# Ten pieces of the first mixer's input projection as 512-column products, with the halves joined in SBUF

## The chip, the cores and the metric

The kernel runs on one core of a Trainium2 chip. The metric is the device time of one execution in microseconds. The core's engines work side by side, each through its own queue in order, and wait for one another by semaphores: TensorE (PE) multiplies, VectorE (DVE) and ScalarE (ACT) work elementwise, GpSimd (POOL) does little here, SyncE (SP) issues the DMAs. PE writes to PSUM alone, which has eight banks of 512 float32 columns; in the programs they are called ps0 to ps7.

## The reference

Three residual blocks over 256 tokens of width 1024. What the change touches is the input projection of the first block's mixer:

```python
h = rmsnorm(x, norm_mix_g[i])
u = h @ w_in[i]
u_rwkv, u_attn, u_gate = jnp.split(u, [RWKV_COLS, RWKV_COLS + ATTN_COLS], axis=-1)
o_a = rwkv7_time_mix(u_rwkv, ...)   # first: c = c + (prev - c) * mu, over tokens
o_b = diff_attention(u_attn, ...)   # q * head_dim ** -0.5, k, v
g_a, g_b = jnp.split(jax.nn.sigmoid(u_gate), 2, axis=-1)
x = x + (g_a * (o_a @ w_proj_a[i]) + g_b * (o_b @ w_proj_b[i])) @ w_out[i]
```

`u_rwkv` has 1792 columns (r, k, v, the decay's, a's and gate's inner parts), `u_attn` 1536 (q, k, v), `u_gate` 2048. All is float32. After the mixer come a squared-ReLU feed-forward, a gate, and then two layers of SwiGLU feed-forward and attention.

## The kernel before

**Precision and weights.** A float32 matrix is split into a high part (ACT rounds it to PE's faster float32 form, L2581) and a low part (DVE subtracts, L2927). Every product is three: high by high, high by low, low by high. The weights come as a stream of pieces of 1 MB; three buffers each hold the raw piece, its high and its low part. A piece's cast waits until PE has used the piece three places before it, and its load until that one's low part is made.

**The stage.** `w_in` is done first in ten and one pieces of 256 columns, whose result is transposed (columns on partitions, tokens along the row): seven pieces for the RWKV inputs in the order of `RWKV_ORDER`, then four for q and k of the differential attention. The first has a form of its own. Each of the others is done by `cols_piece` (L666): 8 steps of contraction x 2 groups of 128 columns x 3 products of 256 tokens (L2072 high by high, L2073 weights' high by tokens' low, L2074 weights' low by tokens' high), all in one PSUM bank of 2 x 256. After every two steps of contraction it yields, so other work may stand there in PE's queue. Then follow v and the gates by `rows_mat` (512-column products with the tokens as the stationary side), and `w_proj_b`.

**Behind a piece.** Of an RWKV piece, DVE scales the bank by the tokens' norm into a buffer (`shift`, L3054), ACT writes the part of the token itself (`shift_old`, L2627 and L2628), and DVE adds the shifted part (`shift_add`, L3058 and L3059), after which `c_ready` counts one. Of a q or k piece, DVE scales the bank (`dqk`). From the first piece ACT makes the decay's inner part (`lora_in`, two table loads), PE two pairs of small products (`lora`, L2273 and L2274), ACT eight sigmoids of them (`lora_out`, L2640 and L2641). When three pieces are ready, ACT squares and copies the keys (`kk`, L2658 and L2662), and PE sums them over heads (`kk_sum`, L2282). From all that follows the RWKV chain: scores, products of 64 x 64, states, outputs.

**The order.** The program is written by generators. `weave` (L1120) runs them as tracks and takes the one whose engine is free first by a table of expected durations; `mixers_fill`, the projections, is the track that fills in. `take` hands out the PSUM bank that has been given back longest ago, and `give` returns it once its reader has been written down; on the chip the next writer then waits for that reader:

```python
def claim(sl):
    if sl.n > 1:
        e.wait_ge(free[sl.b], sl.n - 1)
```

**The wide form.** The feed-forward pieces are done by `wide_runs` (L713): one product of 512 columns takes the weights' high part against the tokens' high and low parts side by side (L2157), which fills a bank, and one of 256 adds the low weights (L2164). A piece takes two banks; its 32 products stand in PE's queue without a break: every other piece has 16 wide ones first and then its low ones, the pieces between begin with two wide ones. In the feed-forward stage ACT then copies one half of each bank to SBUF (L2777) and DVE adds the other half to it (L2920).

Of the kernel before, what the change touches and what calls it, by code (L numbers as in the profile page):

```python
# [14 lines left out]
S = 256  # L15
# [17 lines left out]
LEAD = 10.0  # L33
# [187 lines left out]
def program(nc, ws, xin, pin, colsin, constin, smallin, rowin, out):  # L221
# [4 lines left out]
    with ExitStack() as ctx:  # L226
        def sem(name):
            return ctx.enter_context(nc.semaphore(name))
# [28 lines left out]
        diag_ready = Sig(sem("diag_ready"))  # L257
        c_part = Sig(sem("c_part"))
# [1074 lines left out]


# [217 lines left out]
        def diff():  # L1552
            while "vd" not in state or "bonus" not in state:
                yield None
# [59 lines left out]

        def shifts():

            for n in range(len(RWKV_ORDER)):
                while len(to_shift) <= n:
                    yield None
                p, c, sl, at = to_shift[n]  # L1620
# [4 lines left out]
                emit("shift_old", act=0.83, slot=sl, c=c, i=p % 2, v=c_part.add())  # L1625
                yield "dve"
                emit("shift_add", dve=0.7, c=c, i=p % 2, v_part=c_part.n, v=c_ready.add())

        def mixers_fill(nm):
            for p, c in enumerate(RWKV_ORDER):  # L1630
                def shift(sl, c, nxt, p=p):
                    early.append((p, c, sl, cur[0]))
# [12 lines left out]

            def dq(sl, c, nxt):
                emit("dqk", dve=0.7, slot=sl, n=(c - 1792) // 128)
                if nxt:
                    emit_lo(nxt)
                state["dk"] = sl  # L1650

            for c in range(1792, 2816, 256):
                yield from cols_piece("w_in", 0, c, "h", nm.h_needs, dq)
# [39 lines left out]
        weave([shifts(), rwkv_decays(), rwkv_keys(), (rwkv_chain(), LEAD), (rwkv_block(0), LEAD), (rwkv_block(1), LEAD),  # L1693
# [359 lines left out]
        def tensor_program(e):  # L2053
# [27 lines left out]
            for s in script:  # L2081
# [349 lines left out]
                elif kind == "d_soft":  # L2431
# [3 lines left out]
                    if h == 0:  # L2435
                        read_out(state["dk"])
# [112 lines left out]
        def scalar_program(e):  # L2549
# [20 lines left out]
            for s in script:  # L2570
# [52 lines left out]

                elif kind == "shift_old":
                    read_out(sl)
# [256 lines left out]
        def vector_program(e):  # L2882
# [31 lines left out]

            def add_halves(s, to):
# [17 lines left out]
            for s in script:  # L2933
# [117 lines left out]
                elif kind == "shift":  # L3051
                    c, u_ = s["c"] // 128, ub[s["i"]]
                    ready(sl)
                    e.tensor_tensor(u_[:, :, 1:S + 1], b2(sl), RB2, ALU.mult).then_inc(free[sl.b], 1)  # L3054
# [206 lines left out]
                elif kind == "dqk":  # L3261
                    n = s["n"]
                    ready(sl)
                    if n < 4:
                        e.scalar_tensor_tensor(qT[:, n:n + 2, :], b2(sl), 0.125, RB2, ALU.mult,
                                               ALU.mult).then_inc(free[sl.b], 1)
                    else:
                        e.tensor_tensor(kTt[:, n - 4:n - 2, :], b2(sl), RB2, ALU.mult).then_inc(free[sl.b], 1)
# [381 lines left out]
```

## Time and profile before

| what | value |
|---|---|
| median of 3 runs | 1420.3 us (1419.92 to 1421.13) |
| the profiled execution | 1420.28 us |
| its span in the trace | 1418.5 us |
| PE busy | 1412.6 us, 9224 products |
| DVE, ACT busy | 1128.3 and 803.4 us |

The span runs from the first to the last instruction that the trace has. Products overlap in PE's pipeline, so what one costs is the distance of two starts, not its own length. "Idle" in the trace is time in which an engine had nothing in it; a row that has it names the engine that ended it.

### The profile page before, as it was taken

How to read it: one execution, taken by the hardware profiler on the slowest of the kernel's cores; microseconds unless marked ns; L12 is line 12 of the kernel's file. 1: busy time of each engine (PE TensorE's matmuls, PEld its weight loads, DVE VectorE, ACT ScalarE, POOL GpSimd, SP SyncE). 2: the span in 40 equal slices, each digit the busy share in tenths (PEclk: the TensorE clock that was granted, in tenths of full speed). 3: DMA queues.
4: the chain of work that ended last, by engine and by line, in shares of the span. 5: the costliest groups of instructions: out<-in, count | busy, mean ns of one | idle time of the engine just before them, and what ended most of it. 6: DMA issues, size and time to landing. Idle time of an engine off the chain costs nothing.

```text
span 1418.5 us, 22820 instructions
## 1 busy us (share of the span) xinstructions
PE 1412.6 (100%) x9224; PEld 1203.5 (85%) x9224; DVE 1128.3 (80%) x1543; ACT 803.4 (57%) x1084; POOL 26.3 (2%) x93
## 2 busy tenths in 40 slices
PE   9999999999999999999999999999999999999999
PEld 8988778888888888889878888888888887888887
DVE  6876776786448898888877888889888798688896
ACT  7735473654336565545866565555554557665552
POOL 0000000000001100000000000000000000000000
PEclk9999999999999999999999999999999999999999
DMA  9441325555554555555434555645555444355553
GB/s 339 149 150 62 113 102 204 201 204 187 203 178 179 179 198 189 178 207 178 150 119 166 190 189 188 218 161 199 200 183 193 165 177 149 110 202 194 181 179 115
DMA packets 36104, 249.11 MB, mean 176 GB/s; under 512 B 4128, under 2 KB 4256, under 8 KB 6688
## 3 DMA queue, kind: packets, MB, share of 16 engines
q1 hardware_dynamic: 35712, 247.46, 49.7%
q8 instruction: 74, 1.21, 0.4%
q10 hardware_dynamic: 288, 0.19, 0.1%
q14 instruction: 30, 0.25, 0.1%
HBM read 246.59 MB, written 1.05 MB: 175 GB/s over the span
## 4 chain that ended last, share of the span: by engine, by line
PE 97%; DMA 1%; ACT 1%; DVE 1%; issue 0%; SPq 0%; DVEq 0%; ACTq 0%
PE ps L2157 24%; PE ps L2072 16%; PE ps L2074 16%; PE ps L2073 16%; PE ps L2164 13%; PE ps L2147 2%; PE ps L2332 2%; DMA raw<-ws 1%; PE ps L2146 1%; PE ps L2246 1%; PE ps L2545 1%; PE ps L2525 1%; PE ps L2534 1%; PE ps L2317 0%; ACT hi L2581 0%; PE ps L2469 0%
## 5 line engine op out<-in xcount | busy, mean ns | idle before, releaser
L2927 DVE TENSOR_TENSOR lo<-raw,hi 128x2048 fp32r<-128x2048 f32 (+1 forms) x230 | 525.1, 2283 | 109.9 <-ACT hi L2581 106.9
L2581 ACT CAST hi<-raw 128x2048 fp32r<-128x2048 f32 (+1 forms) x230 | 438.6, 1908 | 205.5 <-PE ps L2074 143.0
L2157 PE MATMUL ps<-h,hi 128*128 128x512 f32 x1504 | 359.2, 390 | 0.0
L2157 PEld LDWEIGHTS ps<-h,hi 128*128 128x128 f32 x1504 | 276.4, 188 | 52.4
L2072 PE MATMUL ps<-hi,a 128*128 128x512 f32 x552 | 218.6, 396 | 0.0
L2074 PE MATMUL ps<-hi,a 128*128 128x512 f32 x552 | 215.4, 390 | 0.0
L2073 PE MATMUL ps<-lo,a 128*128 128x512 f32 x552 | 215.1, 390 | 0.0
L2164 PEld LDWEIGHTS ps<-h,lo 128*128 128x128 f32 x1504 | 192.2, 190 | 7.9
L2164 PE MATMUL ps<-h,lo 128*128 128x256 f32 x1504 | 194.4, 282 | 0.0
L2777 ACT COPY a<-ps 128x256 f32<-128x256 f32 x208 | 76.4, 372 | 178.3 <-PE ps L2157 89.2
L2072 PEld LDWEIGHTS ps<-hi,a 128*128 128x128 f32 x552 | 103.7, 188 | 22.9 <-issue 2.4
L2074 PEld LDWEIGHTS ps<-hi,a 128*128 128x128 f32 x552 | 103.6, 188 | 22.0
L2073 PEld LDWEIGHTS ps<-lo,a 128*128 128x128 f32 x552 | 103.8, 188 | 20.7
L2072 PE MATMUL ps<-hi,h 128*128 128x512 f32 x272 | 112.0, 412 | 0.0
L2074 PE MATMUL ps<-hi,h 128*128 128x512 f32 x272 | 106.3, 391 | 0.0
L2073 PE MATMUL ps<-lo,h 128*128 128x512 f32 x272 | 106.2, 390 | 0.0
L2920 DVE TENSOR_TENSOR a<-ps,a 128x256 f32<-128x256 f32 x208 | 82.6, 420 | 18.7 <-ACT a L2777 16.8
L2072 PE MATMUL ps<-h,hi 128*128 128x256 f32 x224 | 64.8, 289 | 0.4 <-DVE lo L2927 0.4
L2073 PE MATMUL ps<-h,hi 128*128 128x256 f32 x224 | 63.4, 283 | 0.0
L2074 PE MATMUL ps<-h,lo 128*128 128x256 f32 x224 | 63.3, 283 | 0.0
L2072 PEld LDWEIGHTS ps<-hi,h 128*128 128x128 f32 x272 | 51.1, 188 | 12.2 <-issue 2.3
L2074 PEld LDWEIGHTS ps<-hi,h 128*128 128x128 f32 x272 | 51.1, 188 | 11.1
(385 smaller groups left out, 1713.7 us busy)
## 6 DMA issues: line engine op xcount, KB each, us to landing
raw<-ws SPq DMA_DIRECT2D x229, 1024.0 KB, 4.8
X<-xin SPq DMA_DIRECT2D x8, 256.0 KB, 5.3
raw<-ws SPq DMA_DIRECT2D x2, 512.0 KB, 6.2
out<-X SPq DMA_DIRECT2D x4, 256.0 KB, 2.1
small<-small SPq DMA_DIRECT2D x1, 992.5 KB, 12.3
const<-const SPq DMA_DIRECT2D x1, 900.0 KB, 6.6
a<-row SPq DMA_DIRECT2D x1, 512.0 KB, 7.2
const<-const SPq DMA_DIRECT2D x1, 388.0 KB, 12.7
```

The costliest lines, as they stand in the source:

```text
L2072: e.matmul(o, ah, bh, start=start, stop=False)
L2073: e.matmul(o, ah, bl, start=False, stop=False)
L2074: return e.matmul(o, al, bh, start=False, stop=stop)
L2146: e.matmul(b2(sl)[:, 0, :], wl[:, k, a:a + 128], HH[:, k, :], start=False, stop=False)
L2147: t = e.matmul(b2(sl), wh[:, k, a:a + 128], h2[:, k, :, :], start=False, stop=k == 7)
L2157: t = e.matmul(b2(s["slots"][u]), wh[:, k, 128 * u:128 * u + 128], h2[:, k, :, :], start=k == 0, stop=last)
L2164: t = e.matmul(b2(s["slots"][u])[:, 0, :], wl[:, k, 128 * u:128 * u + 128], HH[:, k, :], start=False, stop=last)
L2332: t = e.matmul(banks[z.b][half(q ^ n), 64 * h:64 * h + 64], TB[blk][l][half(q), h, :], TB[blk][r][half(q), h, :], start=True, stop=True)
L2581: e.copy(hi[j % NSPL][:, n], raw[j % NRAW][:, n]).then_inc(hi_ready, 1)
L2777: e.copy(half_to[s["to"]][s["j"]][:, s["u"], :], b2(sl)[:, 1, :]).then_inc(half_a.sem, 1)
L2920: e.tensor_tensor(to[:, u, :], b2(x)[:, 0, :], half_to[kind][j][:, u, :], ALU.add).then_inc(free[x.b], 1)
L2927: e.tensor_tensor(lo[j % NSPL][:, n], raw[j % NRAW][:, n], hi[j % NSPL][:, n].bitcast(F), ALU.subtract).then_inc(lo_ready, 1)
```

## The change

Ten pieces, all RWKV ones but the first and the four of q and k, go from `cols_piece` to `wide_runs`. Their results lie in two banks as two halves each. A new step `halves` (ACT, L2667 of the changed kernel) copies the second half of each bank into one of two buffers `hv`; `meet_halves` (DVE, L2963) adds the first half, which frees the bank; the scaling by the tokens' norm is then done in SBUF (L3107, L3323). `shift_old` waits for a new semaphore, `piece_scaled`. The buffers `hv` share their place with some of the RWKV chain's, so the chain's blocks may be written down only after the last piece of k (`"dk"`), and so may the differential attention.

```diff
+        hv_ar = Arena(vend + 3 * 16 * S)
+        hv = [hv_ar([128, 2, S]) for _ in range(2)]
...
         def rwkv_block(blk):
+            while "dk" not in state:
+                yield None
...
+        def halves_out(n, slots, at):
+
+            yield "act", at
+            emit("halves", act=0.9, slots=slots, i=n % 2, over=state.get(("hv", n % 2)), v=[half_a.add() for _ in slots])
+            halves = script[-1]["v"]
+            state["hv", n % 2] = slots[1]
+            return halves
...
+        def queries():
+
+            for n in range(4):
+                while len(to_scale) <= n:
+                    yield None
+                c, sl, other, at = to_scale[n]
+                halves = yield from halves_out(7 + n, (other, sl), at)
+                yield "dve"
+                emit("dqk", dve=1.4, slot=sl, other=other, halves=halves, i=(7 + n) % 2, n=(c - 1792) // 128, v=scaled_v.add())
+                for x in (other, sl):
+                    give(x)
+            state["dk"] = scaled_v.n
...
-                yield "dve", at
-                emit("shift", dve=0.55, slot=sl, c=c, i=p % 2)
-                give(sl)
+                p, c, sl, other, at = to_shift[n]
+                halves = None
+                if other:
+                    halves = yield from halves_out(p, (other, sl), at)
+                    yield "dve"
+                else:
+                    yield "dve", at
+                emit("shift", dve=1.35 if other else 0.55, slot=sl, other=other, halves=halves, c=c, i=p % 2, v=scaled_v.add())
...
-                    yield from cols_piece("w_in", 0, c, "h", nm.h_needs, shift)
+                    yield from wide_runs("w_in", 0, c, nm.h_needs, no_begin, shift)
...
-                yield from cols_piece("w_in", 0, c, "h", nm.h_needs, dq)
+                yield from wide_runs("w_in", 0, c, nm.h_needs, no_begin, dq)
...
-        weave([shifts(), rwkv_decays(), rwkv_keys(), (rwkv_chain(), LEAD), (rwkv_block(0), LEAD), (rwkv_block(1), LEAD),
+        weave([shifts(), queries(), rwkv_decays(), rwkv_keys(), (rwkv_chain(), LEAD), (rwkv_block(0), LEAD), (rwkv_block(1), LEAD),
...
+                elif kind == "halves":
+                    if s["over"]:
+                        read_out(s["over"])
+                    for u, x in enumerate(s["slots"]):
+                        ready(x)
+                        e.copy(hv[s["i"]][:, u, :], b2(x)[:, 1, :]).then_inc(half_a.sem, 1)
                 elif kind == "shift_old":
-                    read_out(sl)
+                    e.wait_ge(scaled_v.sem, s["scaled"])
...
+            def meet_halves(s, to):
+
+                for u, x in enumerate((s["other"], s["slot"])):
+                    e.wait_ge(half_a.sem, s["halves"][u])
+                    e.tensor_tensor(to[:, u, :], b2(x)[:, 0, :], hv[s["i"]][:, u, :], ALU.add).then_inc(free[x.b], 1)
+                read_out(s["other"])
+                read_out(s["slot"])
...
+                    if s["other"]:
+                        meet_halves(s, u_)
+                        e.tensor_tensor(u_, u_, RB2, ALU.mult).then_inc(scaled_v.sem, 1)
...
+                    meet_halves(s, t)
+                    e.scalar_tensor_tensor(t, t, 0.125 if n < 4 else 1.0, RB2, ALU.mult, ALU.mult).then_inc(scaled_v.sem, 1)
```

The order of the queues shows it best around the small products of the decay and the keys. PE before, from the first pair of decay products to the first key sum; `small` holds the decay's weights, `a1` the mixed inputs, `a14` the keys' squares:

```order
L2074 MATMUL ps1<-h_59,lo0_55 128x256
L2273 MATMUL ps2<-a1_67,small_62 128x256 [waits const_in,rwkv_act,bank_free3,bank_free2]
L2274 MATMUL ps3<-a1_67,small_62 128x256
...
L2273 MATMUL ps4<-a1_67,small_62 128x256 [waits const_in,rwkv_act,bank_free7,bank_free4]
L2274 MATMUL ps7<-a1_67,small_62 128x256
...
L2282 MATMUL ps2<-a14_80,const_61 128x256 [waits rwkv_keys,bank_free2]
L2072 MATMUL ps6<-h_59,hi2_54 128x256
```

PE now, from the end of piece 3 to the start of piece 5:

```order
L2202 MATMUL ps4<-h_59,lo0_55 128x256 x8
L2311 MATMUL ps0<-a1_67,small_62 128x256 [waits const_in,rwkv_act,bank_free5,bank_free0]
L2312 MATMUL ps5<-a1_67,small_62 128x256
...
L2195 MATMUL ps6<-h_59,hi1_53 128x512 [waits hi_ready,bank_free7,bank_free6]
...
L2195 MATMUL ps7<-h_59,hi1_53 128x512 x7
L2311 MATMUL ps1<-a1_67,small_62 128x256 [waits const_in,rwkv_act,bank_free2,bank_free1]
L2312 MATMUL ps2<-a1_67,small_62 128x256
...
L2320 MATMUL ps0<-a14_80,const_61 128x256 [waits rwkv_keys,bank_free0]
...
L2195 MATMUL ps5<-h_59,hi2_54 128x512 [waits hi_ready,bank_free3,bank_free5]
```

Before, the pairs of decay products stand two steps of contraction apart, inside piece 3, and the key sums two pieces later inside piece 5. Now a whole piece lies between the pairs, and the first key sum follows the second pair at once, in the first pair's bank.

ACT before, from the cast of piece 5 to the squares of the keys; `hi` are casts, `a9` and `a12` the sigmoids of the decay products:

```order
L2581 CAST hi2_54<-raw2_51 128x2048 [waits bank_full0,raw_in2]
L2627 ACTIVATE a1_67<-a3_69,st_63 128x256 [waits bank_free6]
L2640 ACTIVATE a9_75<-ps2,cols_60 128x256 [waits bank_full3]
...
L2641 ACTIVATE a12_78<-ps7,cols_60 128x256
L2627 ACTIVATE a1_67<-a2_68,st_63 128x256 [waits bank_free0]
...
L2581 CAST hi0_52<-raw0_49 128x2048 [waits bank_full1,raw_in0]
...
L2658 ACTIVATE a14_80<-a1_67,st_63 128x256 [waits c_ready]
```

ACT now, from the same cast to the sigmoids:

```order
L2619 CAST hi2_54<-raw2_51 128x2048 [waits bank_full2,raw_in2]
L2671 ACTIVATE a1_67<-a3_69,st_63 128x256 [waits piece_scaled]
...
L2619 CAST hi0_52<-raw0_49 128x2048 [waits bank_full4,raw_in0]
L2667 COPY a33_99<-ps1 128x256 [waits bank_full1]
...
L2671 ACTIVATE a1_67<-a2_68,st_63 128x256 [waits piece_scaled]
...
L2702 ACTIVATE a14_80<-a1_67,st_63 128x256 [waits c_ready]
...
L2619 CAST hi1_53<-raw1_50 128x2048 [waits bank_full7,raw_in1]
L2667 COPY a34_100<-ps3 128x256 [waits bank_full3,bank_free7]
...
L2684 ACTIVATE a9_75<-ps0,cols_60 128x256 [waits bank_full5]
L2685 ACTIVATE a12_78<-ps5,cols_60 128x256
```

The eight sigmoids stood ahead of the casts of the pieces 6 and 7 and ahead of the keys' squares and copies; now they stand behind all of these.

## Rows read from the trace of the kernel before

**Rows 1.** The page: busy times, and the granted clock in 40 slices.
```profile
PE 1412.6 (100%) x9224; PEld 1203.5 (85%) x9224; DVE 1128.3 (80%) x1543; ACT 803.4 (57%) x1084; POOL 26.3 (2%) x93
...
PEclk9999999999999999999999999999999999999999
```

**Rows 2.** Waits of PE, 12 to 200 us: us in total, times, longest.
```profile
PE ps L2072 <- DVE lo L2927: 0.4, 1, 0.4
PE ps L2273 <- ACT a L2633: 0.2, 1, 0.2
```

**Rows 3.** Windows: us; PE, PEld, DVE, ACT, POOL busy; clock, DMA share, GB/s.
```profile
16.00:84.00 68.00, 67.36 (x640) 65.20 (x641) 54.42 (x70) 46.95 (x63) 2.24 (x9) 1.00 0.57 203
```

**Rows 4.** Timeline of PE in piece 2: start, length in us, what.
```profile
23.09 0.28 PE L2072 MATMUL ps<-h,hi 128*128 128x256 f32 x1
...
29.81 0.28 PE L2074 MATMUL ps<-h,lo 128*128 128x256 f32 x1
```

**Rows 5.** Timeline of PE in the first feed-forward stage.
```profile
289.71 6.99 PE L2157 MATMUL ps<-h,hi 128*128 128x512 f32 x30
296.54 2.08 PE L2164 MATMUL ps<-h,lo 128*128 128x256 f32 x16
298.45 0.63 PE L2157 MATMUL ps<-h,hi 128*128 128x512 f32 x2
```

**Rows 6.** Timeline of PE: start of piece 1, first decay products, and behind.
```profile
16.43 0.38 PE L2072 MATMUL ps<-h,hi 128*128 128x256 f32 x1 [0.43 <-DVE lo L2927]
...
30.30 0.45 PE L2273 MATMUL ps<-a,small 64*128 64x256 f32 x1 [0.21 <-ACT a L2633]
...
31.36 0.39 PE L2072 MATMUL ps<-h,hi 128*128 128x256 f32 x1
```

**Rows 7.** The page's groups: busy us, mean ns, idle before.
```profile
L2777 ACT COPY a<-ps 128x256 f32<-128x256 f32 x208 | 76.4, 372 | 178.3 <-PE ps L2157 89.2
...
L2920 DVE TENSOR_TENSOR a<-ps,a 128x256 f32<-128x256 f32 x208 | 82.6, 420 | 18.7 <-ACT a L2777 16.8
```

**Rows 8.** Timeline of DVE behind the pieces 1 and 2.
```profile
29.74 0.69 DVE L3054 TENSOR_TENSOR a<-ps,RB 128x512 f32<-128x512 f32 x1
...
34.19 0.48 DVE L3058 SCALAR_TENSOR_TENSOR a<-a,cols,a 128x256 f32<-128x256 f32 x1
...
34.98 0.68 DVE L3054 TENSOR_TENSOR a<-ps,RB 128x512 f32<-128x512 f32 x1
```

**Rows 9.** Timeline of DVE in the first feed-forward stage.
```profile
291.12 0.69 DVE L3304 TENSOR_TENSOR a<-a,a 128x512 fp32r<-128x512 f32 x1 [0.69 <-ACT a L2781]
```

**Rows 10.** Timeline of ACT, 24 to 48 us.
```profile
25.80 0.51 ACT L2627 ACTIVATE a<-a,st 128x256 f32<-128x256 f32 x1
...
26.73 1.28 ACT L2632 ACT_TABLE_LOAD   x1
...
30.06 1.88 ACT L2581 CAST hi<-raw 128x2048 fp32r<-128x2048 f32 x1
31.85 0.51 ACT L2627 ACTIVATE a<-a,st 128x256 f32<-128x256 f32 x1
...
32.66 0.45 ACT L2640 ACTIVATE a<-ps,cols 128x256 f32<-128x256 f32 x1
33.02 0.46 ACT L2641 ACTIVATE a<-ps,cols 128x256 f32<-128x256 f32 x1
...
40.61 1.70 ACT L2658 ACTIVATE a<-a,st 128x256 f32<-128x256 f32 x4
...
43.81 1.89 ACT L2581 CAST hi<-raw 128x2048 fp32r<-128x2048 f32 x1
```

**Rows 11.** Timeline of the program's first PE work.
```profile
1.44 3.78 PE L2079 MATMUL ps<-lo 128*128 128x512 f32 x8 [1.44 <-DVE lo L2932]
...
10.02 0.28 PE L2100 MATMUL ps<-h,hi 128*128 128x256 f32 x1
...
10.13 0.28 PE L2101 MATMUL ps<-h,hi 128*128 128x256 f32 x1
```

More of the change, by code:

```diff
@@ L257, in program @@
         diag_ready = Sig(sem("diag_ready"))
+        scaled_v = Sig(sem("piece_scaled"))
         c_part = Sig(sem("c_part"))
@@ L1552, in diff @@
         def diff():
-            while "vd" not in state or "bonus" not in state:
+            while "vd" not in state or "bonus" not in state or "dk" not in state:
                 yield None
@@ L1619, in shifts, with no_begin, shift @@
                     yield None
-                p, c, sl, at = to_shift[n]
-                yield "dve", at
-                emit("shift", dve=0.55, slot=sl, c=c, i=p % 2)
-                give(sl)
+                p, c, sl, other, at = to_shift[n]
[6 more added lines that the diff above has]
+                emit("shift", dve=1.35 if other else 0.55, slot=sl, other=other, halves=halves, c=c, i=p % 2, v=scaled_v.add())
+                scaled = scaled_v.n
+                for x in (other, sl):
+                    if x:
+                        give(x)
                 yield "act"
-                emit("shift_old", act=0.83, slot=sl, c=c, i=p % 2, v=c_part.add())
+                emit("shift_old", act=0.83, scaled=scaled, c=c, i=p % 2, v=c_part.add())
                 yield "dve"
                 emit("shift_add", dve=0.7, c=c, i=p % 2, v_part=c_part.n, v=c_ready.add())
+        def no_begin(sl, c, u):
+            pass
         def mixers_fill(nm):
             for p, c in enumerate(RWKV_ORDER):
-                def shift(sl, c, nxt, p=p):
-                    early.append((p, c, sl, cur[0]))
+                def shift(sl, c, nxt, other=None, p=p):
+                    early.append((p, c, sl, other, cur[0]))
                     if p == 1:
@@ L1643, in mixers_fill, with dq @@
                 else:
-                    yield from cols_piece("w_in", 0, c, "h", nm.h_needs, shift)
[L1646 to L1650, printed above, removed]
+                    yield from wide_runs("w_in", 0, c, nm.h_needs, no_begin, shift)
+            def dq(sl, c, nxt, other):
+                to_scale.append((c, sl, other, cur[0]))
+                emit_lo(nxt)
+                return True
             for c in range(1792, 2816, 256):
-                yield from cols_piece("w_in", 0, c, "h", nm.h_needs, dq)
+                yield from wide_runs("w_in", 0, c, nm.h_needs, no_begin, dq)
             def vd(sl, b, h):
@@ L3051, in vector_program @@
                 elif kind == "shift":
-                    c, u_ = s["c"] // 128, ub[s["i"]]
-                    ready(sl)
-                    e.tensor_tensor(u_[:, :, 1:S + 1], b2(sl), RB2, ALU.mult).then_inc(free[sl.b], 1)
+                    c, u_ = s["c"] // 128, ub[s["i"]][:, :, 1:S + 1]
+                    if s["other"]:
+                        meet_halves(s, u_)
+                        e.tensor_tensor(u_, u_, RB2, ALU.mult).then_inc(scaled_v.sem, 1)
+                    else:
+                        ready(sl)
+                        e.tensor_tensor(u_, b2(sl), RB2, ALU.mult).then_inc(free[sl.b], 1)
+                        read_out(sl)
+                        e.sem_inc(scaled_v.sem, 1)
                 elif kind == "shift_add":
@@ L3262, in vector_program @@
                     n = s["n"]
[L3263 to L3268, printed above, removed]
+                    t = qT[:, n:n + 2, :] if n < 4 else kTt[:, n - 4:n - 2, :]
+                    meet_halves(s, t)
+                    e.scalar_tensor_tensor(t, t, 0.125 if n < 4 else 1.0, RB2, ALU.mult, ALU.mult).then_inc(scaled_v.sem, 1)
                 elif kind == "gate_in":
```

3 lines of the change are left out of this document (2 added, 1 removed).

## The prediction

> **What bounds the kernel now.** I read the page's busy times first, then TensorE's (PE's) waits, then the stage that is changed, then the lengths of single operations there. PE is busy in 1412.6 of 1418.5 us, and no slice of the granted clock is below its highest digit [rows 1]. Between 12 and 200 us, which holds the whole changed stage, PE waited 0.6 us in all: 0.4 for a low part of the weights and 0.2 for ScalarE (ACT) [rows 2]. So PE has no slack that could swallow a new wait: a microsecond that PE waits in this stage ends up in the total, and one that its products lose comes off it. VectorE (DVE) was busy 54.4 and ACT 47.0 of the 68 us from 16 to 84 [rows 3]; there the ten pieces lie.
>
> The profiled execution took 1420.28 us with a span of 1418.5; it lies 0.02 under the median of the runs, 1420.3, so the sum is made on 1420.3. A difference under 0.2% (2.8 us, so 1417.5 to 1423.1) can't be told from none.
>
> **What PE gains.** A piece of before is 48 products of 256 columns. Their starts lie 0.12 us apart (57 of them, of which the first and the last stand in [rows 4]: 6.72 us over 56 steps), 5.76 us a piece. The new form is that of the feed-forward pieces of the same kernel: 30 products of 512 columns in 6.83 us are 0.228 each, and 16 of 256 in 1.91 us are 0.119 each [rows 5]; 16 of either are 5.55 us. That is 0.21 us a piece and 2.1 us for ten. Two more waits go: piece 1 started with the low weights missing (0.4 us idle, [rows 6]) and now begins with its high products, which were cast before; and the 0.2 us before the first small product of the decays [rows 6], because PE will come to it later. Piece 2 must then wait some 0.1 to 0.2 us for its low weights, which I leave inside the rounding. Gain: 2.7 us, with bounds of 2 (the waits come back elsewhere) and 3.4 (0.1 us, by which the first product behind a small one is longer, 0.39 against 0.28 [rows 4, 6], for each of some seven places where none cuts a piece any more).
>
> **What DVE and ACT pay.** A piece now has its two halves in two banks. ACT copies one half of each bank (2 x 0.37 us by the row of the same copy in the feed-forward stage, [rows 7]), DVE adds the other half (2 x 0.42, the same rows) and scales afterwards in SBUF, 0.69 by the row of such a product in SBUF [rows 9], as long as the scaling that it did from PSUM [rows 8]. Ten pieces: 7.4 us on ACT, 8.4 on DVE. Neither is on the path by its length alone: DVE comes to about 63 of the 65 us that the stretch then has. It matters through the order in which each engine must take its work.
>
> **The wait that comes in.** A piece was four or more interruptible steps and is now one block of 5.55 us, so small products come only between pieces, and a piece holds two of the eight PSUM banks instead of one. By the order of the program, the first key sum (L2320) now stands right behind the second pair of decay products, and is written to bank 0, the bank of the first pair. Bank 0 comes free when ACT has done the third of the eight activations L2684/L2685. Before, the key sums had banks 2 and 3, which had long been read.
>
> When does PE get there? At 30.30 less 0.2 us idle [rows 6] PE had done pieces 1, 2 and a quarter of 3. The rest of piece 3 takes 4.3 us at the old pitch, which gives 34.4; less the 0.4 us at the start and three times 0.21 it is 33.4. A pair of decay products takes 1.06 us (30.30 to 31.36, [rows 6]): 34.4. Piece 4, whose parts are ready, ends at 40.0, the second pair at 41.0.
>
> When is bank 0 free? ACT works without a break from 25.80 [rows 10], in its new order: scaled copy 0.93 (to 26.73, as before), halves 0.74, the step with two table loads 3.33 (26.73 to 30.06), cast 1.79 (30.06 to 31.85), scaled copy 0.81, cast 1.79, halves 0.74: 35.9. DVE is by then waiting for these halves: one add 0.42 [rows 7] and the scaling 0.69 [rows 9]: 37.0. ACT's scaled copy 0.93: 38.0; DVE's two sums 0.85 (34.19 to 34.98 plus some of the second's tail, [rows 8]): 38.8. Only then may ACT begin the keys' squares and copies, 3.20 (40.61 to 43.81, [rows 10]): 42.0. Ahead of the decay activations stand one more cast, 1.79, and one more pair of halves, 0.74: 44.5. Three activations at 0.36 a step, the last 0.45 long [rows 10]: 45.7. PE waits from 41.0 to 45.7: **4.7 us**. Bounds from the same rows: 4.0, if the second of each pair of copies costs only the 0.36 step that ACT shows between short activations and PE comes later by what its gain misses; 5.5, if each handover between engines costs 0.1 more.
>
> What is queued behind it: everything on PE, pieces 5 to 10. Who waits for them: the casts of pieces 8 and on, which need the weights' buffer back. They don't come late: with PE late by 4.7 us, DVE and ACT catch up, and by the same walk piece 8's low weights are ready 5 us or more ahead.
>
> **The next tight places.** By the same walk PE ends piece 10 near 81. The low parts of the pieces 11 and 12 come about 1 and 0.4 us before PE wants them, and the last sum of the seven, for which the first turn of v waits, about 0.5 us after. I take 0.5, bounds 0 and 2. Then the RWKV chain: its first scores come near 90 instead of 69 us, because its buffers share SBUF with the new halves, and until then nothing of it stands in PE's queue. But the products that fill its waits are consumed earlier too. No row shows how little filling the chain can do with; PE waited for none of it before [rows 2]. I take 0.5 us, bounds 0 and 4, near the lower end because that row is the nearest one.
>
> **Sum:** 1420.3 - 2.7 + 4.7 + 0.5 + 0.5 = 1423.3. The rest of the program is the same but for the banks' numbers.
>
> **Rivals.**
> *The clock falls in the wait.* PE would stand still for almost 5 us. The trace before has its clock at the higher level throughout [rows 1], but also no idle stretch of that length to tell. At the start of the program, PE's first eight products of 512 columns take 3.78 us [rows 11], 0.47 each against 0.233 in [rows 5] (6.99 us for 30): that is the lower level of 1.2 GHz, after PE had done nothing. If the level falls in the wait, the products behind it run at twice their step for a while. Eight products at the low level lost 8 x 0.24 = 1.9 us, which bounds the price from below; 8.6 us after the first of them the products of 256 columns have their full step of 0.11 to 0.12 [rows 11], so at most half of that, 4.3 us, is lost. I take 2.5, near the lower end, because PE ran other work at that level in between: 1425.8.
> The Trainium skill ("TensorE: Matmul & The Clock Gate", section "What's actually happening") says that the throttled level is the default and activity releases it, so a pause can put it back. By that rule the time would be this rival's; the start agrees (0.47 against 0.233), a pause inside the kernel no row here shows.
>
> *The wait isn't there: faster, or the same.* The place is the release of bank 0. If ACT reached the decay activations before 41.0, PE would keep its whole gain: 1417.6, or up to 0.7 less. From 43.7 on the gain is used up; that is the point from which it decides. For it: PE has so far never waited in this stage although the planner that ordered it has the same work to hide. Against it: ACT takes its queue in order, and its own work from 25.80 to the third activation sums to 18.0 us, so that it would end at 43.8 even if it never waited for DVE, just where the gain is used up; the two waits for DVE, 0.42 + 0.69 and 0.85, bring the 45.7.
>
> *DVE becomes the bound.* It is at 80% in this stretch [rows 3] and would be at some 96%. If of its 13.6 us of waiting there half stayed, because adds and casts wait for one another in order, its low parts would be late by some 4 us more, on top of the wait: 1427.5. For it: ever more of its work waits for a half that ACT copies behind a cast. Against: scores, masks and kappa, some of the 54.4 us, leave the stretch, since the chain starts after it.
>
> *The chain runs dry.* Fewer filling products lie in it: 1425 to 1428 with the bounds above.
>
> **How the numbers follow.** The sum's own case has 0.46, with 1421 to 1425.5 from the bounds of its wait and gain; about half of it lies above 1423.1. The clock 0.24, at 1424 to 1428. The missing wait 0.14, at 1417 to 1420; half of it, 0.07, under 1417.5. DVE's bound and the dry chain together 0.16, at 1425 to 1431. So slower 0.22 + 0.24 + 0.16, and a little off for the cases' lower ends: 0.59; faster 0.08; the same 0.33. For the range one in ten may be left out on either side: the lower end goes into the missing wait, 1418.8, the upper through the clock's case to 1428.0. I name 1423.3.
>
> **What would show it.** In the profile after, PE is idle some 4.7 us before the first L2320, at about 41 to 46 us, and the activation L2684 ends just before it goes on. The 512-column products L2195 keep the 0.228 step in this stage, and a piece lasts 5.55. PE waits little before pieces 5 to 10. If the clock fell, the slice of the granted clock around 46 us falls and the 512-column products there take twice their step. The forecast is wrong if there is no idle time before L2320, if the first scores come before 85 us, or if PE's waits from 90 to 200 us add up to more than 2 us.

## The result and the profile after

| | before | changed |
|---|---|---|
| median of 6 runs | 1420.68 us (1419.92 to 1421.13) | 1427.78 us (1427.12 to 1428.79) |
| ratio of the two, 95% interval | | 1.0050 (1.0039 to 1.0061) |
| the profiled execution, its span | 1420.28, 1418.5 us | 1427.57, 1425.5 us |

The changed kernel is slower by 7.1 us. That is in the forecast's range, whose upper end was 1428.0, but 4.5 us above the time it named.

**Where it sits.** By PE's timelines the transposition of the mixer's result (L2291, before L2253) starts at 216.28 us before and at 223.29 in the changed kernel; from there to its last product PE takes 1198.9 us in the one and 1198.8 in the other. So all 7.0 us of the profiled executions lie in the changed stage and the RWKV chain behind it. The line that answers to [rows 3], and PE's waits, which answer to [rows 2] (changed kernel; the columns are as there):

```profile
16.00:84.00 68.00, 62.95 (x355) 54.18 (x354) 53.46 (x70) 50.48 (x79) 2.25 (x9) 0.97 0.52 193
```
```profile
PE ps L2320 <- ACT a L2684: 4.6, 1, 4.6
PE ps L2284 <- DMA X<-xin: 0.9, 1, 0.9
PE ps L2370 <- DVE st L2956: 0.8, 1, 0.8
PE ps L2327 <- DVE a L3117: 0.7, 1, 0.7
PE ps L2370 <- DVE a L3192: 0.7, 2, 0.4
PE ps L2202 <- DVE lo L2979: 0.4, 1, 0.4
```

The first line of the waits is the forecast one: the key sum L2320, released by ACT's L2684. The last is piece 1's wait of [rows 6], which has only moved to piece 2. L2327 is the first turn of v, and the two of L2370 are products of the chain, between 109 and 121 us.

Here is ACT's queue ahead of that key sum, in the changed kernel's timeline (start, length, what); it answers to [rows 10]:

```profile
34.32 1.91 ACT L2619 CAST hi<-raw 128x2048 fp32r<-128x2048 f32 x1 [1.10 <-PE ps L2202]
...
39.98 1.71 ACT L2702 ACTIVATE a<-a,st 128x256 f32<-128x256 f32 x4 [0.95 <-DVE a L3117]
41.59 1.69 ACT L2706 ACTIVATE a<-a,st 128x256 f32<-128x256 f32 x4
43.19 1.88 ACT L2619 CAST hi<-raw 128x2048 fp32r<-128x2048 f32 x1
44.98 0.63 ACT L2667 COPY a<-ps 128x256 f32<-128x256 f32 x2
45.50 0.47 ACT L2684 ACTIVATE a<-ps,cols 128x256 f32<-128x256 f32 x1
45.87 0.46 ACT L2685 ACTIVATE a<-ps,cols 128x256 f32<-128x256 f32 x1
46.23 0.47 ACT L2684 ACTIVATE a<-ps,cols 128x256 f32<-128x256 f32 x1
```

The first line is a cast that had to wait for PE. From 39.98 on, the keys' squares and copies (L2702, L2706) come first, then a cast and two halves, and only then the eight evictions of the decay products (L2684, L2685). Before, these began at 32.66 and the keys at 40.61 [rows 10]. The third eviction ends at 46.70, and PE goes on at 46.75. PE's rows from there show two more things:

```profile
46.75 2.08 PE L2320 MATMUL ps<-a,const 128*128 128x256 f32 x4 [4.61 <-ACT a L2684]
48.26 4.84 PE L2195 MATMUL ps<-h,hi 128*128 128x512 f32 x16
52.94 2.07 PE L2202 MATMUL ps<-h,lo 128*128 128x256 f32 x16
54.85 1.02 PE L2320 MATMUL ps<-a,const 128*128 128x256 f32 x4
55.52 0.82 PE L2195 MATMUL ps<-h,hi 128*128 128x512 f32 x2
56.18 2.06 PE L2202 MATMUL ps<-h,lo 128*128 128x256 f32 x16
58.08 6.99 PE L2195 MATMUL ps<-h,hi 128*128 128x512 f32 x30
...
83.49 0.39 PE L2110 MATMUL ps<-hi,h 128*128 128x512 f32 x1
```

First, the wide form keeps its step: 30 products from 58.08 to 64.90 are 0.227 us each, and five pieces (6 to 10) take from 55.52 to 83.49, 5.59 each, against 5.55 forecast [rows 5] and 5.76 before [rows 4]. Second, the first 16 wide products after the wait took 4.68 us (48.26 to 52.94) instead of 3.64, and the first four key sums 1.51 (46.75 to 48.26) instead of 0.67 (54.85 to 55.52): 1.9 us lost. The clock column of the windows (changed kernel, columns as in [rows 3]) says why:

```profile
40.00:46.50 6.50, 2.14 (x13) 1.25 (x11) 3.54 (x2) 6.50 (x14) 0.00 (x0) 1.00 0.45 164
46.50:50.00 3.50, 3.25 (x8) 2.60 (x9) 3.40 (x7) 3.11 (x9) 0.00 (x0) 0.51 0.41 119
```

The granted clock is 1.00 until 46.5 and 0.51 from 46.5 to 50.0 us: its lower level, 1.2 of 2.4 GHz, right behind the idle time. (The page's row of the clock, in which I expected to see it, shows nothing: its slices are 36 us long and read 9 as in [rows 1].) This was the rival *the clock falls in the wait*. The rule named there (the Trainium skill, "TensorE: Matmul & The Clock Gate", section "What's actually happening") agrees with this trace: 4.61 us without work, then 0.51. Behind other waits in the runs below the clock did not fall.

By these rows the sum is: wait 4.6, clock 1.9, v's turn 0.7, chain 1.5, later start 0.2 (PE came to piece 1 at 16.24, before at 16.43 less 0.43 idle, [rows 6]; the tokens' DMA, the line with xin, was late), and a gain of 10 x 0.17 + 0.2 = 1.9. That is 7.0, as measured. It adds up, but the experiments show that the wait is not a price by itself: e11 and e9, with less of it or none, end no earlier by their medians.

### The profile page after: what moved, and what is told of

Read it like the earlier page. It is cut to its first block, busy times and chain, and to the rows that moved or that the text cites. A ratio compares the mean times of both kernels' runs of the same rounds, so it can differ in the third digit from the quotient of the medians.

```text
span 1425.5 us, 22560 instructions
## 1 busy us (share of the span) xinstructions
PE 1411.9 (99%) x9064; PEld 1194.7 (84%) x9064; DVE 1135.8 (80%) x1563; ACT 809.6 (57%) x1104; POOL 26.6 (2%) x93
## 3 DMA queue, kind: packets, MB, share of 16 engines
q1 hardware_dynamic: 35712, 247.46, 48.5%
## 4 chain that ended last, share of the span: by engine, by line
PE 95%; DVE 2%; ACT 1%; DMA 1%; issue 1%; SPq 0%; POOL 0%; DVEq 0%; ACTq 0%; POOLq 0%
PE ps L2195 26%; PE ps L2110 15%; PE ps L2112 14%; PE ps L2111 14%; PE ps L2202 14%; PE ps L2185 2%; PE ps L2370 1%; PE ps L2184 1%; PE ps L2284 1%; PE ps L2583 1%; DVE lo L2979 1%; ACT hi L2619 1%; DMA raw<-ws 1%; PE ps L2563 1%; PE ps L2572 1%
## 5 line engine op out<-in xcount | busy, mean ns | idle before, releaser
L2195 PE MATMUL ps<-h,hi 128*128 128x512 f32 x1664 | 399.1, 391 | 0.0
L2195 PEld LDWEIGHTS ps<-h,hi 128*128 128x128 f32 x1664 | 306.4, 189 | 58.6 <-issue 0.3
L2202 PEld LDWEIGHTS ps<-h,lo 128*128 128x128 f32 x1664 | 212.6, 190 | 9.5 <-DVE lo L2979 0.9
L2202 PE MATMUL ps<-h,lo 128*128 128x256 f32 x1664 | 215.2, 282 | 0.4 <-DVE lo L2979 0.4
L2635 ACT CAST h<-nt 128x512 fp32r<-128x512 f32 x36 | 22.2, 620 | 65.6 <-DVE nt L3051 65.3
L2111 PEld LDWEIGHTS ps<-lo,h 128*128 128x128 f32 x272 | 51.2, 188 | 8.5
L2185 PE MATMUL ps<-h,hi 128*128 128x512 f32 x140 | 50.2, 395 | 0.0
```

The costliest lines, as they stand in the source:

```text
L2111: e.matmul(o, ah, bl, start=False, stop=False)
L2185: t = e.matmul(b2(sl), wh[:, k, a:a + 128], h2[:, k, :, :], start=False, stop=k == 7)
L2195: t = e.matmul(b2(s["slots"][u]), wh[:, k, 128 * u:128 * u + 128], h2[:, k, :, :], start=k == 0, stop=last)
L2202: t = e.matmul(b2(s["slots"][u])[:, 0, :], wl[:, k, 128 * u:128 * u + 128], HH[:, k, :], start=False, stop=last)
L2635: e.copy(HH[:, 4 * h:4 * h + 4, 128 * b:128 * b + 128], n4[s["n"] % 2]).then_inc(h_hi.sem, 1)
```

## Experiments on the wait and the clock

Each run was timed beside the kernel before on the same chip (medians of 1420.6 to 1420.8 us). Ratios are to it, with 95% intervals. In these kernels, line numbers are up to 4 higher than in the changed one.

**The idle time cut in two (e1_split_idle).** 1427.82 us, ratio 1.0050 (1.0037 to 1.0062).

```diff
                     e.wait_ge(rwkv_a.sem, rwkv_a.at["lora_in"])
+                    if s["c2"] == 1:
+                        e.wait_ge(rwkv_k.sem, rwkv_k.at["kk0"])
```


> The changed kernel, in which the second pair of low-rank products waits until ACT has made the last of the eight scaled keys (43.3 us in its trace); nothing else waits for them before ACT's 46.2 us, so the 4.6 us in which TensorE stands before the first key sum is cut in two, about 1.6 and 2.6 us, with its sum and everything behind it where it was. If the clock fell because of one long idle stretch, the fall to 1.2 GHz at 46.6 us (3.4 us long, so 1.7 us of work lost) does not come, and the kernel takes about 1426.1 us, 1.7 less than the changed one. If the clock falls for another reason, or its fall cost nothing at the end, it stays at 1427.8.

PE's waits are now 2.4 and 1.7 us, about as intended. But the clock fell all the same, and stayed low for longer (this run's window):

```profile
43.30:50.20 6.90, 5.19 (x17) 3.63 (x14) 5.61 (x8) 6.51 (x14) 0.00 (x0) 0.51 0.65 241
```

So one long idle stretch isn't needed, and this run doesn't price the clock.

**The keys' copies later on ACT (e11_copies_later).** 1429.92 us, ratio 1.0061 (1.0048 to 1.0073).

```diff
-            rwkv_k.mark("sq0", "sq1", "kk0")
-            emit("kk", act=3.2)
+            rwkv_k.mark("sq0", "sq1")
+            emit("kk", act=1.6)
...
+            rwkv_k.mark("kk0")
+            emit("kk_scaled", act=1.6)
+            yield "act"
             rwkv_k.mark("rn")
```


> The changed kernel, in which ACT makes the four squares of the keys where it did, and the four scaled copies of them (1.65 us) only before the root; all other work is the same. Nothing needs the copies before the normalisation. Theory (the first key sum waits for what stands ahead of the evictions on ACT): the wait becomes some 1 us at the first key sum and 1.5 us at the fifth piece, the clock may not fall, 1423 to 1426 us. Rival (banks are short whatever ACT does first): the idle time of TensorE between 41 and 50 us stays above 4 us in sum, and the time at 1427 to 1429 us.

This run decides against my sum. Its profiled execution took 1427.47 us, the same as the changed kernel's 1427.57. Yet the wait before the key sums is mostly gone, and the clock never fell in it. (The other four executions have a mean granted clock of 0.997 to 0.999 and took 1428.9 to 1430.7 us, so the clock did fall in those; all six of the changed kernel have 0.998 or 0.999.) PE's waits in the profiled one:

```profile
PE ps L2373 <- ACT a L2737: 3.1, 1, 3.1
PE ps L2198 <- issue: 1.5, 1, 1.5
PE ps L2330 <- DVE a L3121: 1.5, 1, 1.5
PE ps L2198 <- DVE a L2967: 1.4, 1, 1.4
PE ps L2373 <- ACT a L2734: 1.3, 1, 1.3
```

At the first key sum 0.55 us are left (its row has 42.05 as its start), and before the fifth piece 1.5, much as the theory had it; but its time did not come. For v's turn (L2330) now waits 1.5, a later wide piece 1.4, and the chain's products (L2373) 3.1 and 1.3. The idle time has changed its place. The same shows when PE's idle time is summed by stretch. The first number is the stretch, the second its length, the third PE's busy time; the last stretch ends where the mixer's output products are done. Before, changed, and this run:

```profile
16.00:60.00 44.00, 43.36 (x350) 42.13 (x351) 33.57 (x43) 38.71 (x55) 2.24 (x9) 1.00 0.68 247
60.00:84.00 24.00, 24.00 (x292) 23.07 (x292) 20.85 (x27) 8.23 (x8) 0.00 (x0) 1.00 0.36 123
84.00:216.28 132.28, 132.01 (x2042) 105.14 (x2041) 91.77 (x186) 73.36 (x130) 0.00 (x0) 1.00 0.31 108
```
```profile
16.00:60.00 44.00, 38.95 (x219) 33.05 (x218) 33.60 (x46) 34.47 (x55) 2.25 (x9) 0.96 0.59 224
60.00:84.00 24.00, 24.00 (x138) 21.12 (x137) 19.86 (x24) 16.01 (x25) 0.00 (x0) 1.00 0.41 137
84.00:223.29 139.29, 136.60 (x2171) 108.42 (x2170) 101.06 (x206) 76.44 (x136) 0.00 (x0) 1.00 0.30 107
```
```profile
16.00:60.00 44.00, 41.49 (x235) 34.95 (x234) 35.06 (x49) 34.53 (x54) 2.25 (x9) 1.00 0.66 249
60.00:84.00 24.00, 22.59 (x130) 19.86 (x129) 20.33 (x24) 17.33 (x26) 0.00 (x0) 1.00 0.37 132
84.00:223.47 139.47, 132.20 (x2159) 106.33 (x2158) 98.81 (x204) 74.68 (x134) 0.00 (x0) 1.00 0.28 101
```

Length less PE: 0.6 + 0 + 0.3 = 0.9 us idle before; 5.1 + 0 + 2.7 = 7.7 in the changed kernel; 2.5 + 1.4 + 7.3 = 11.2 here. (Ends of products are modelled, so such a sum is good to a microsecond or two.) The 2.5 us that the first stretch won are lost behind 60 us, and more.

**Evictions right after each pair (e9_out_at_once).** 1429.66 us, ratio 1.0062 (1.0049 to 1.0074).

```diff
                 lora.append((bw, ba))
-            for c2, (bw, ba) in enumerate(lora):
                 yield "act"
                 emit("lora_out", act=1.45, c2=c2, bw=bw, ba=ba)
```


> The changed kernel, in which ACT is given the evictions of each low-rank pair right after that pair, and not those of both pairs after the second; the first pair's banks come free before ACT makes the scaled keys, the second pair uses them again, and the planner then puts the key sums behind the sixth piece. Theory (bank order costs 4.6 us and the clock's fall 1.7): no wait over 1 us between 16 and 84 us, the clock stays at 2.4 GHz, 1421.5 to 1423.5 us, most of the remaining loss being the chain's 0.9 and 2.0 us. Rival (the key sums come some 9 us later, and VectorE's products of the chain with them, so the wait reappears in the chain or at a later piece's banks, as it did when both pairs were issued together): 1425 to 1430 us, with a wait of 2 to 4 us on a bank that VectorE holds.

The rival held, with a wait of 4.6 us where it had 2 to 4. The key sums themselves no longer wait, but the piece behind them does, for as long as the key sum did, and the clock fell there too (0.95 over 60 to 84 us). PE, and DVE at the same time:

```profile
59.19 1.19 PE L2195 MATMUL ps<-h,hi 128*128 128x512 f32 x2 [4.62 <-issue]
```
```profile
55.61 0.68 DVE L3137 TENSOR_SCALAR a<-ps 128x512 f32<-128x512 f32 x1
56.21 2.28 DVE L2979 TENSOR_TENSOR lo<-raw,hi 128x2048 fp32r<-128x2048 f32 x1
58.41 0.68 DVE L3137 TENSOR_SCALAR a<-ps 128x512 f32<-128x512 f32 x1
```

Piece 7 is written to the two banks of the key sums. L3137 empties them, and its second instruction stands behind a low cast of 2.28 us; it ends at 59.09.

**Both pairs ahead of piece 4 (e2_pairs), and with buffers of their own (e4_pairs_own).** 1433.68 us, ratio 1.0090 (1.0077 to 1.0104), and 1428.81, ratio 1.0059 (1.0046 to 1.0073).

```diff
+            yield "pe"
+            yield from room(4)
             for c2 in range(2):
-                yield "pe"
-                yield from room(2)
                 bw, ba = take(), take()
```


> The changed kernel with both pairs of low-rank products issued together ahead of the fourth wide piece, so that ACT empties their banks before it makes the scaled keys. Theory (the loss is ACT's order, in which eight bank evictions and the scaled keys stand ahead of the bank that the first key sum takes): TensorE's 4.6 us before the first key sum fall to under 2 us, the clock does not fall (1.7 us), and the kernel takes 1421.5 to 1424 us. Rival (all eight banks are full in this stretch whatever the order, because a wide piece holds two): the idle time moves to the fourth or fifth piece at the same length and the time stays within 1 us of 1427.8.

> Both of these edits together: low-rank products issued together, and the halves in buffers of their own. If the two causes are apart, the gains add: the time of the run with the pairs alone, less what the buffers alone took off, 1420 to 1423 us. If the late chain was a result of the idle TensorE and not of the buffers, it is the time of the run with the pairs alone within 0.4 us.

Neither expectation of e2_pairs held: it is worse than the rival. The evictions end at 39.1 us, but piece 4 waits for their banks, a later piece (at 73.7 us) waits for halves that DVE joins behind long instructions of the chain, and the longest wait comes at 188 us, at the chain's far end:

```profile
PE ps L2499 <- issue: 3.1, 1, 3.1
PE ps L2195 <- DVE a L2963: 2.9, 1, 2.9
PE ps L2195 <- ACT a L2684: 2.2, 1, 2.2
```

**Buffers of their own (e3_own_buffers).** 1431.51 us, ratio 1.0080 (1.0068 to 1.0093).

```diff
-        hv_ar = Arena(vend + 3 * 16 * S)
-        hv = [hv_ar([128, 2, S]) for _ in range(2)]
+        hv = [nt[1 - i][:, :].rearrange("p (u n) -> p u n", u=2) for i in range(2)]
...
-            while "dk" not in state:
-                yield None
```


> The changed kernel with the eviction buffers of the halves in the two buffers of the norm, which nothing else uses at that time, so that the RWKV blocks no longer have to be planned behind the last of the differential keys; first scores and triangle products then stand right behind piece 10, among the first products of the values, instead of some 6 us later. Theory (the chain is late because of the shared buffers and has less fill at its end): the waits of 0.4, 0.9, 0.5 and 0.4 us between 109 and 168 us shrink and the kernel takes 1425.5 to 1427 us. Rival one (the chain's waits come from VectorE's added work, 0.7 us a piece): within 0.4 us of 1427.8. Rival two (with the scores earlier they wait for VectorE's products, which come at 83 to 92 us): 1428 to 1430 us.

The first scores came at 83.4 instead of 93.8 us, and the kernel became 3.7 us slower, above the range of rival two as well: taking away the gate that I held for part of the harm gains nothing in this order. In e4_pairs_own the same edit comes with a kernel 4.9 us faster than e2_pairs, so its effect depends on the order around it, the two edits don't add, and neither expectation of e4_pairs_own held.

## Experiments on the pieces

These kernels use the wide form for some pieces only; which ones stands in the heading. The others go through `cols_piece` and are scaled from PSUM in one step, as before.

**Queries and keys alone (e6_qk_wide):** 1421.22 us, ratio 1.0004 (0.9995 to 1.0013). **All RWKV pieces, no queries and keys (e7_rwkv_wide):** 1427.84, ratio 1.0049 (1.0036 to 1.0061).

```diff
-                    yield from wide_runs("w_in", 0, c, nm.h_needs, no_begin, shift)
+                    yield from cols_piece("w_in", 0, c, "h", nm.h_needs, shift)
```
(e6; in e7 the same swap stands in the loop over queries and keys.)

> Only the four pieces of differential queries and keys in 512-column products with their halves joined in SBUF; the six RWKV pieces in 256-column products as in the kernel before. Theory (the loss sits where the first key sum finds all banks taken, 4.6 us, in the clock that falls there, 1.7 us, and a smaller part of about 3 us in the late chain): no wait before the key sums and no fall of the clock, the gain of four pieces is 4 x 0.21 = 0.8 us; with the late chain in full 1420.7 - 0.8 + 2.9 = 1422.8 us, without it 1419.9 us; so 1419.5 to 1423. Rival (VectorE's added 0.7 us a piece and the planner's other order cost by themselves, wherever they are): 1423 to 1425 us.

> Only the six RWKV pieces wide; the four of differential queries and keys in 256-column products, scaled from PSUM in one step as before. Theory: the wait before the first key sum and the fall of the clock stay (4.6 + 1.7 us), the gain is 6 x 0.21 + 0.6 = 1.9 us, and the chain is late by less because four joinings of halves and the wait for their buffers are gone: 1425 to 1427.5 us. Rival (most of the loss comes through the queries and keys): 1421 to 1424 us.

As far as these two runs can tell, the loss lies in the RWKV pieces, all of it: e7 has the changed kernel's time to 0.1 us (0.3 above its theory's range), and e6 can't be told from before.

**All but the fourth (e10_piece4_narrow):** 1429.14 us, ratio 1.0059 (1.0046 to 1.0072). **Pieces 1 to 3 (e12_first_three):** 1429.03, 1.0058 (1.0045 to 1.0072). **Pieces 1, 2, 3, 6 (e13_three_and_six):** 1427.17, 1.0049 (1.0037 to 1.0062). **Pieces 1 and 2 (e14_first_two):** 1423.79, 1.0026 (1.0017 to 1.0035). In e12 to e14 queries and keys are as before, by the same swap as in e7. The edit of the RWKV loop, for e12:

```diff
-                else:
+                elif p in (1, 2, 3):
                     yield from wide_runs("w_in", 0, c, nm.h_needs, no_begin, shift)
+                else:
+                    yield from cols_piece("w_in", 0, c, "h", nm.h_needs, shift)
```


> The changed kernel, with only the fourth RWKV piece (the one that stands between the two pairs of low-rank products) in 256-column products with one bank each half. The planner can then put the second pair among its products, as before, and the key sums among those of later pieces. Theory (a wide piece is one block of 5.6 us that pushes the second pair, and with it all eight evictions, behind the scaled keys): no wait over 1 us before the key sums and no fall of the clock, the gain of nine wide pieces, about 2.5 us, stays, the late chain's 2.9 us stays: 1420 to 1423 us. Rival (wide pieces hold two banks each for so long that TensorE runs out of banks in this stretch in any order): a wait of 2 to 5 us at a piece or a sum between 40 and 75 us, and 1424 to 1428 us.

> Only the three pieces ahead of the low-rank products wide (pieces 1, 2 and 3), all others in 256-column products. Theory: none of the wide pieces' banks are held when the keys and the chain want them, so of the change only its gain is left, 3 x 0.21 us and 0.6 us at the start of the first: 1419 to 1420.5 us. Rival (the other order of the planner costs the chain about what the pieces gain, as with the queries and keys alone): 1420.5 to 1422.5 us.

> The first three pieces and the sixth wide, pieces 4 and 5 and all queries and keys in 256-column products. Theory: as with the first three, and 0.2 us more: 1418.8 to 1420.3 us. Rival (a wide piece behind the key sums meets ACT's roots and exponentials and VectorE's scans, and waits for banks): 1421 to 1425 us.

> Only pieces 1 and 2 wide, one wide piece fewer than in the run with the first three (1429.0 us). The other runs show that where the loss is, ACT's evictions of the low-rank products, from which the decay chain starts, come late: at 32.7 to 35.7 us in the kernel before and with the queries and keys alone wide (1421.2 us), at 45.5 to 48.5 us in the changed kernel and up to 50.3 us with the first three. Here three pieces hold one bank each half again when the second low-rank pair wants two, and the planner puts both pairs six products apart, as before, with VectorE's scan ahead of the third shift. Theory (the loss of 6 to 8 us begins where the second pair finds no two banks and the evictions slip behind the keys): the evictions end by 39 us, the first key sum waits for nothing over 1 us, and the time is 1419 to 1421.5 us. Rival (each wide RWKV piece ahead of the keys delays the relay of ACT and VectorE by its halves, whatever the order of the evictions): 1424 to 1428 us.

Each of the four missed the theory's time; the first three lie above their rival's range as well, and e14 lies 0.2 us below it. In e10 piece 5 waited 3.9 us at 46.65, and the clock fell there. e12 has no wide piece anywhere near the key sums, and in its profiled execution the clock never fell. Its first key sum still waits for ACT's evictions, now numbered L2688, and then PE waits for low weights that DVE makes late:

```profile
PE ps L2324 <- ACT a L2688: 2.4, 1, 2.4
PE ps L2114 <- DVE lo L2983: 2.3, 2, 1.2
```

e14, with one wide piece less, has no such wait up to 84 us. Its longest wait comes at the end of the mixer, for DVE, and there the clock fell (PE's timeline, then the window behind it):

```profile
213.63 0.60 PE L2114 MATMUL ps<-hi,a 128*128 128x512 f32 x1 [1.89 <-DVE a L3266]
```
```profile
213.80:217.20 3.40, 3.40 (x9) 2.65 (x9) 3.27 (x3) 0.96 (x1) 0.00 (x0) 0.50 0.90 308
```

What these runs have in common is read from the same views: when the last eviction of the decay products ends on ACT, when the scan that starts the decay chain begins on DVE, and PE's idle time from 16 us to the end of the mixer. These three are of the profiled execution, whose time stands beside the median.

| run | median us | profiled us | evictions end | scan begins | PE idle |
|---|---|---|---|---|---|
| before | 1420.7 | 1420.3 | 35.7 | 35.7 | 0.9 |
| e6_qk_wide | 1421.2 | 1421.4 | 35.7 | 36.0 | 4.7 |
| e14_first_two | 1423.8 | 1425.3 | 39.8 | 40.6 | 4.1 |
| e13_three_and_six | 1427.2 | 1427.2 | 50.0 | 51.4 | 7.2 |
| changed | 1427.8 | 1427.6 | 48.5 | 48.8 | 7.7 |
| e1_split_idle | 1427.8 | 1427.3 | 47.9 | 48.2 | 7.3 |
| e7_rwkv_wide | 1427.8 | 1427.8 | 48.0 | 48.3 | 6.4 |
| e4_pairs_own | 1428.8 | 1432.2 | 40.8 | 41.0 | 9.3 |
| e12_first_three | 1429.0 | 1428.8 | 50.3 | 51.7 | 7.7 |
| e10_piece4_narrow | 1429.1 | 1430.1 | 50.7 | 50.8 | 8.0 |
| e9_out_at_once | 1429.7 | 1428.4 | 43.9 | 44.0 | 8.8 |
| e11_copies_later | 1429.9 | 1427.5 | 47.2 | 47.3 | 11.2 |
| e3_own_buffers | 1431.5 | 1431.0 | 48.5 | 48.8 | 10.4 |
| e2_pairs | 1433.7 | 1434.3 | 39.1 | 39.3 | 12.6 |

The scan's rows in the timelines of DVE, of before and of the changed kernel (the other cells of that column are read in the same way):

```profile
35.74 2.44 DVE L3066 TENSOR_TENSOR_SCAN a<-const,a 128x256 f32<-128x256 f32 x4
```
```profile
48.77 2.43 DVE L3124 TENSOR_TENSOR_SCAN a<-const,a 128x256 f32<-128x256 f32 x4
```

Only the two kernels whose scan begins at 36 us are near 1421, and no kernel with a later one comes back to it. But the order isn't strict: e2_pairs starts its scan at 39.3 and is the slowest, and the changed kernel and e3_own_buffers start theirs at 48.8 and lie 3.7 us apart. So a late start of the decay chain goes with the loss, and is not shown to be all of it. Nor is the idle time a price by itself: e6 has 4.7 us of it, and its first scores come at 88.4 us instead of 69.0, for 0.5 us in the median. The other candidate is the longer relay behind each wide piece: two ACT copies and two DVE sums more, in the stretch from 36 to 60 us, where ACT was already busy 22.06 of 24 us before:

```profile
36.00:60.00 24.00, 24.00 (x196) 23.79 (x196) 19.33 (x23) 22.06 (x31) 0.00 (x0) 1.00 0.48 173
```

e14 and e2_pairs speak for the relay: their scans begin 1.3 us apart, with two wide pieces and with ten, and their medians lie 9.9 us apart. But the order of their small products differs too.

What stays open is how the loss divides between the two. A kernel with three wide pieces and the evictions first, and one with pieces 4 to 6 wide and the evictions as before, would tell them apart; they were not run. No version beat the kernel before.

## Why the prediction was right or wrong

**The wait that comes in: right.** 4.6 us against 4.7, at L2320, released by the third L2684, with the first scores late as forecast. The walk through ACT's queue came within a microsecond of the end of that activation (45.7 forecast, 46.70 measured), and PE arrived later by as much, 42.1 instead of 41.0. So both ends were late by a microsecond, and that they cancel is luck. On ACT's side the walk had no break, while the cast at 34.32 (the first line of its queue above) waited 1.10 us for PE to finish piece 3, whose place in the weights' buffers it takes.

**What PE gains: a little too high in the sum.** 1.9 us instead of 2.7: a piece takes 5.59 and not 5.55, and the 0.4 us of piece 1 moved to piece 2 instead of going. This is a reckoning by step. Counted from start to start, without idle time and without what the low clock cost, the ten pieces take some 56.4 us instead of 59.3, because in the kernel before 16 of the starts, most of them beside small products, came some 0.1 us late; about 1 us of these 2.9 is lost again on other products, whose starts lie further apart.

**The clock: a rival that should have been in the sum.** It had 0.24 and came true as described, at 1.9 us instead of 2.5. One of its grounds is weaker than it reads: at the program's start the lower level is inferred from the step of the products alone, while the clock column of the windows reads 1.00 there (0 to 4 us).

**The next tight places: the mis-sized term.** Forecast 0.5 for v's turn and 0.5 for the chain, with bounds 0 to 2 and 0 to 4; the changed kernel waited 0.7 and 1.5. Its own sign of error, waits from 90 to 200 us of over 2 us in all, came true: v's turn and the two lines of L2370 make 2.2. The rival *DVE becomes the bound* did not happen: DVE was busy 53.5 of the 68 us.

**Why 1427.8 still lies in the range.** From 1423.3, the gain adds 0.8, the clock 1.9, the two tight places 1.2 and the later start 0.2; the wait takes off 0.1, and the median of before is now 0.4 higher. The range reached that far only because of the clock's case; that case came with a smaller price than forecast and with larger waits behind it, so the hit is in part luck.

**The step that failed: the sum as a sum.** I took each wait as a price that goes when the wait goes; so the rival *the wait isn't there* stood at 1417.6. e11, e9 and e12 shrink or move this wait, and their medians are 1429.0 to 1429.9 us. By these runs the wait was only the place where the loss first showed on PE. "PE has no slack" held for the waits of the changed kernel, but e6, with 4.7 us idle for 0.5, suggests that not all idle time ends up in the total. My reading, argued and not shown, is this: PE's full queue before was the result of fill laid into the chain's pauses, and a chain whose scan starts 13 us later has that fill behind it already. I also judged DVE and ACT to be off the path "by its length alone" from the 68 us window of [rows 3], in which ACT is at 69%. Its part from 36 to 60 us, shown above, is at 92%, and three of the ten pairs of new copies came there; in the changed kernel it is at 75%, with the work slid to later:

```profile
36.00:60.00 24.00, 19.39 (x105) 16.37 (x104) 18.62 (x25) 18.06 (x35) 0.00 (x0) 0.93 0.36 133
```

## What to carry to other kernels

When a wait is found at the head of a serial chain, ask what a later start of the chain costs at its far end before pricing the wait: taking the wait away may only move it. Read the busy share of the engine that receives new work over the stretch of a few operations where it lands, not over the stage. And try a change of many like parts on the parts that feed no chain first: here four pieces of ten cost nothing measurable, and the other six alone cost as much as all ten.

## What the runs showed of the hardware

The clock fell behind short waits, but not behind every one. It fell behind waits of PE of 2.4 us (e1_split_idle, at 42.82), 1.9 (e14_first_two, at 213.63) and 4.6 (changed kernel). It stayed at 1.00 behind 2.4 us in e12_first_three and behind 3.1 in e11_copies_later (PE's timelines and the windows around them). In e2_pairs it fell behind 2.2 us (at 37.75) and not behind 2.9 (at 73.70):

```profile
46.17 1.13 PE L2324 MATMUL ps<-a,const 128*128 128x256 f32 x4 [2.43 <-ACT a L2688]
```
```profile
43.00:50.00 7.00, 4.57 (x32) 4.16 (x31) 3.13 (x5) 7.00 (x17) 0.00 (x0) 1.00 0.00 1
```
```profile
156.75 1.46 PE L2373 MATMUL ps<-a,a 64*64 64x64 f32 x77 [3.12 <-ACT a L2737]
```
```profile
153.00:160.00 7.00, 3.36 (x153) 2.90 (x149) 5.65 (x17) 4.82 (x14) 0.00 (x0) 1.00 0.41 143
```

So a wait of this length can't be priced from its length alone. It also differs from one execution to the next. Of the 11 executions of e14_first_two, six took 1423.4 to 1423.8 us, each with a mean granted clock of 1.000, and five took 1425.1 to 1425.6, each with 0.998 or 0.999. The profiled one, with the fall, took 1425.3. The medians of the two sets lie 1.8 us apart, and 3.4 us at half the clock lose 1.7. e13_three_and_six divides in the same way: three executions at 1.000 took 1426.7 to 1427.2 us, two at 0.999 took 1429.2 and 1429.5. So the same program keeps its clock in one execution and loses it in another, and the fall has its price in the total. Where it fell in the executions that were not profiled is not shown.
